# Second layer of an eight-stage transformer stack: order of the values' tiles, their copies, two weight blocks and the rotation of the shared keys

## The reference, cut to what matters

```python
def mla_layer(x, norm_g, w_in, q_a_norm, w_uq, kv_a_norm, w_ukv, q_head_norm, k_head_norm, w_out):
    proj = rms_norm(x, norm_g) @ w_in            # 1024 -> 256 + 128 + 64 + 1024
    q_lat, kv_lat, k_pe, gate = ...
    q = (rms_norm(q_lat, q_a_norm) @ w_uq).reshape(B, S, 8, 192)
    kv = (rms_norm(kv_lat, kv_a_norm) @ w_ukv).reshape(B, S, 8, 256)
    k_nope, v = kv[..., :128], kv[..., 128:]
    k = concatenate([k_nope, k_pe for every head])
    q, k = rms_norm(q, q_head_norm), rms_norm(k, k_head_norm)
    q, k = rope on the last 64 of 192 columns
    o = causal_softmax_attention(q, k, v, 1.0 / sqrt(192))
    return x + (o * silu(gate)) @ w_out
```

## Time and profile before

| | us |
|---|---|
| median of 3 runs | 1969.71 (1968.24 to 1970.51) |
| the profiled execution, its own time | 1964.89 |
| its span (first to last instruction) | 1963.1 |
| TensorE busy in it | 1867.9 (95%) |
| VectorE, ScalarE, POOL busy | 967.3, 794.3, 467.8 |
| mean granted TensorE clock | 0.979 |

### The profile page before, as it was taken

One profiled execution on the slowest core, in us unless ns is written; L12 is line 12 of the kernel. 1 busy time (PEld: TensorE's weight loads), 2 busy tenths in 40 slices (PEclk: granted clock), 3 DMA queues, 4 the chain that ended last, 5 costly groups with the idle time before them and its releaser, 6 DMA issues.

```text
span 1963.1 us, 24562 instructions
## 1 busy us (share of the span) xinstructions
PE 1867.9 (95%) x9682; PEld 1465.6 (75%) x9682; DVE 967.3 (49%) x1575; ACT 794.3 (40%) x1397; POOL 467.8 (24%) x471
## 2 busy tenths in 40 slices
PE   6999989999999989999999999999998999999997
PEld 5987777765677756667888888877877788888885
DVE  5345564575446577744533333354555353333334
ACT  4235663454435355554442323233444334232322
POOL 0035551101312124541120201005556302010200
PEclk9999999998999989999999999999999799999998
DMA  4321111221012310001223222221111023222231
GB/s 152 97 76 52 49 38 56 88 72 54 1 54 84 124 54 23 23 23 54 87 97 103 98 87 96 97 86 54 65 55 55 23 86 107 97 95 98 88 103 66
DMA packets 40289, 143.32 MB, mean 73 GB/s; under 512 B 4592, under 2 KB 4976, under 8 KB 40176
## 3 DMA queue, kind: packets, MB, share of 16 engines
q1 hardware_dynamic: 40176, 141.76, 21.9%
HBM read 139.64 MB, written 2.10 MB: 72 GB/s over the span
## 4 chain that ended last, share of the span: by engine, by line
PE 85%; DVE 5%; ACT 4%; POOL 3%; issue 2%; DMA 1%; DVEq 0%; SPq 0%; ACTq 0%; POOLq 0%
PE BANK L275 22%; PE BANK L277 21%; PE BANK L276 21%; PE BANK L856 3%; PE BANK L629 2%; PE BANK L1618 2%; PE BANK L1575 1%; PE BANK L1599 1%; ACT WH L252 1%; PE BANK L913 1%; DVE LH L719 1%; PE BANK L2357 1%; PE BANK L614 1%; PE BANK L2382 1%; PE BANK L2304 1%
## 5 line engine op out<-in xcount | busy, mean ns | idle before, releaser
L252 ACT ACTIVATE WH<-WRAW 128x1024 fp32r<-128x1024 f32 x262 | 273.5, 1045 | 487.2 <-PE BANK L277 448.3
L261 DVE TENSOR_TENSOR WL<-WRAW,WH 128x1024 fp32r<-128x1024 f32 (+1 forms) x249 | 325.2, 1306 | 269.8 <-ACT WH L252 269.7
L275 PE MATMUL BANK<-HH,WH 128*128 128x512 f32 x1048 | 426.5, 407 | 20.8 <-DVE WL L261 18.1
L277 PE MATMUL BANK<-HL,WH 128*128 128x512 f32 x1048 | 410.1, 391 | 0.0
L276 PE MATMUL BANK<-HH,WL 128*128 128x512 f32 x1048 | 409.7, 391 | 0.0
L275 PEld LDWEIGHTS BANK<-HH,WH 128*128 128x128 f32 x1048 | 197.8, 189 | 71.1 <-ACT WH L252 18.8
L276 PEld LDWEIGHTS BANK<-HH,WL 128*128 128x128 f32 x1048 | 198.1, 189 | 43.1 <-issue 5.3
L277 PEld LDWEIGHTS BANK<-HL,WH 128*128 128x128 f32 x1048 | 197.6, 189 | 42.5
L2245 POOL TENSOR_TENSOR HID<-TMP,HID 128x512 fp32r<-128x512 f32 x64 | 83.0, 1297 | 532.4 <-ACT HID L2226 532.4
L277 PE MATMUL BANK<-HID,WH 128*128 128x512 f32 x512 | 202.2, 395 | 0.0
L275 PE MATMUL BANK<-HID,WH 128*128 128x512 f32 x512 | 202.2, 395 | 0.0
(11 more groups left out here) (387 smaller groups left out, 3153.4 us busy)
## 6 DMA issues: line engine op xcount, KB each, us to landing
WRAW<-in_w SPq DMA_DIRECT2D x77, 512.0 KB, 3.4
WRAW<-in_wu SPq DMA_DIRECT2D x64, 512.0 KB, 3.2
WRAW<-in_wd SPq DMA_DIRECT2D x64, 512.0 KB, 3.2
WRAW<-in_w0o SPq DMA_DIRECT2D x8, 512.0 KB, 3.4
WRAW<-in_w1o SPq DMA_DIRECT2D x8, 512.0 KB, 3.5
WRAW<-in_wc SPq DMA_DIRECT2D x8, 512.0 KB, 3.3
WRAW<-in_w2o SPq DMA_DIRECT2D x8, 512.0 KB, 3.2
WRAW<-in_w3o SPq DMA_DIRECT2D x8, 512.0 KB, 3.3
```

Source lines behind the costliest of these rows:

```text
L252: e.activation(WH[b % NS][:, 0:n], WRAW[b % NR][:, 0:n], ACT.Copy).then_inc(*inc("s_high", ("high", b)))
L261: e.tensor_tensor(WL[b % NS][:, 0:n], WRAW[b % NR][:, 0:n], WH[b % NS][:, 0:n].bitcast(F32), ALU.subtract).then_inc(*inc("s_low_pool" if p ...
L275: e.matmul(dst, ah, bh, start=first and i == 0, stop=False)
L277: made = e.matmul(dst, ah, bl, start=False, stop=last and i == len(sets) - 1)
```

## The change

Six edits, all in the second layer.

1. `k rot` holds bank 7 in place of the ring's next, and the ring is one of seven banks from there on (before: from the first query tile on). All tiles behind it lie one bank further back than before.
2. VectorE turns the shared keys (`rope(("k",), ...)`) after the four evictions of `queries(0)` in place of before the evictions of the key tiles.
3. The values' tiles hold banks 0 to 7 in their own order; the ring's count is moved by 13 in place of 4, so that the output tiles lie where they lay.
4. VectorE copies the values' tiles 0, 2, 4 and 6, ScalarE 1, 3, 5 and 7, after the silus and the table load.
5. The splits of `m_o` 1 and `m_o` 2 move from ahead of the attention steps to the end of their steps 9 and 13, on both engines.
6. The first product with the values waits for the copies of tiles 6 and 7, as there are two copying engines now.

```diff
+        m_late = {9: "m_g", 13: "m_v"}
...
-            bank, was = banks.take("k rot", ("k sin",))
+            bank, was = banks.hold("k rot", 7, ("k sin",))
+            banks.ring = range(7)
...
-            banks.ring = range(7)
             queries(0)
...
-                    bank, was = banks.take(("m_v", 2 * i + half), ("evac", "m_v", 2 * i + half))
+                    bank, was = banks.hold(("m_v", 2 * i + half), 2 * i + half, ("evac", "m_v", 2 * i + half))
...
-            banks.i += 4
+            banks.i += 13
...
                     if step == 7:
+                        w.wait_ge(*at("evac", "m_v", 6))
                         w.wait_ge(*at("evac", "m_v", 7))
...
-            rope(("k",), "k rot", mkpe)
             for m in range(0, 8, 2):
                 w.wait_ge(*at("tile", "m_k", m))
                 e.tensor_copy(mkn[:, m, :], banks["m_k", m]).then_inc(*inc("s_evac", ("evac", "m_k", m)))
...
             queries(0)
+            rope(("k",), "k rot", mkpe)
             gate(2)
...
-            gate(7)
-            for m in range(8):
+            by_rs(e, w, "m_g", 7, mlg[:, 7, :])
+            for m in range(0, 8, 2):
                 w.wait_ge(*at("tile", "m_v", 7 if m == 6 else m))
-                e.tensor_copy(mv[:, m // 2, 512 * (m % 2):512 * (m % 2) + 512], banks["m_v", m]).then_inc(
-                    *inc("s_evac", ("evac", "m_v", m)))
-            split_low(e, w, after_block("m_v", 0), False)
+                e.tensor_copy(mv[:, m // 2, 0:512], banks["m_v", m]).then_inc(*inc("s_evac", ("evac", "m_v", m)))
...
+                if step in m_late:
+                    split_low(e, w, after_block(m_late[step], 7 if step == 9 else 0), False)
...
-            split_high(e, w, after_block("m_g", 7))
             silu(7)
             e.preload_act_table_set("natural_log_exp_and_others")
-            split_high(e, w, after_block("m_v", 0))
+            for m in range(1, 8, 2):
+                w.wait_ge(*at("tile", "m_v", m))
+                e.activation(mv[:, m // 2, 512:1024], banks["m_v", m], ACT.Copy).then_inc(
+                    *inc("s_evac_act", ("evac", "m_v", m)))
...
+                if step in m_late:
+                    split_high(e, w, after_block(m_late[step], 7 if step == 9 else 0))
```

## The result

| | before | after |
|---|---|---|
| median us | 1968.97 (4 runs, 1968.16 to 1970.51) | 1958.90 (4 runs, 1957.71 to 1960.55) |
| ratio | | 0.9949, 95% interval 0.9931 to 0.9966 |
| the profiled execution, its own time; span | 1964.89; 1963.1 | 1960.55; 1958.8 |
| mean granted clock | 0.979 | 0.979 |

The change makes the kernel 10 us faster, 0.5%; 8.8 us were forecast, with a time of 1961.0 us. In a later session it measured 1959.50 us (11 runs), ratio 0.9956, interval 0.9940 to 0.9972.

A forecast was written before the change was run, and what follows sets the result against it. TensorE, busy for 95% of the span, was taken to lose time only by standing still and by the lower clock. 0.9 + 1.2 + 6.7 = 8.8 us won gave 1961.0 us, 8-in-10 range 1956.5 to 1968.2.

The forecast's parts named there:

- What bounds it: Second layer's attention: TensorE stalls 1.52 us ahead of the scores, then runs 13.5 us at granted clock 0.50.
- Rotation and key tiles: Ahead of the first query tile: a 2.38 us stall goes, 0.6 and 0.9 us waits come; 0.9 us won.
- Values' tiles: Ahead of the first scores: the 1.52 us stall goes, the second tile loses 0.3 us; 1.2 us won.
- Clock: In the first scores: without the stall the clock stays at 1.00, halving 13.5 us of work; 6.7 us won.
- Late splits: At attention steps 9 and 13: the moved splits hide behind TensorE's other work; cost 0, bounds 0 to 0.5 each.
- Sum: Whole kernel: 0.9 + 1.2 + 6.7 = 8.8 us won, for a time of 1961.0 us.
- rule on bank cycling: Rival at the key tiles: the new waits cost the clock, giving 1962.6 or 1967.7 us; chance 0.10.
- The rival of later stalls: Stalls after this stage come 8.8 us earlier and together lose over 4 us of clock; chance 0.06.

The follow-up runs named there:

- `p2_values`: Before, with values' tiles on banks 0 to 7, copied by VectorE and ScalarE; both splits still ahead of the steps: 1958.57 us, ratio 0.9948.
- `p3_late`: Before, with only the two splits moved to the end of steps 9 and 13; banks and VectorE's eight copies unchanged: 1959.41 us, ratio 0.9960.
- `p4_fill`: Before, plus seven bf16 matmuls of 512 columns, changing no result, in the stall ahead of the scores: 1959.68 us, ratio 0.9958.
- `q3_stall2`: Changed kernel with a 1.9 us stall put back ahead of the scores, by two further copies on ScalarE: 1967.19 us, ratio 1.0006.
- `q1_nokeys`: Changed kernel with the rotation product back on the ring of eight and the shared keys turned before the key copies: 1960.47 us, ratio 0.9969.
- `p1_keys`: Before, with only the rotation product on bank 7, the ring of seven and the later turning of shared keys: 1966.64 us, ratio 0.9990.
- `q2_stall0`: Changed kernel with a 0.7 us stall ahead of the scores, waiting for the copy of values' tile 7: 1958.91 us, ratio 0.9952.
- `s1_both9`: Changed kernel with both late splits at step 9 instead of steps 9 and 13: 1958.24 us, ratio 0.9960.
- `r_after`: The changed kernel once more, unaltered, beside its variants on one chip: 1959.50 us, ratio 0.9956.
- `b2_early`: Changed kernel, ring shifted so no tile of the layer's first half lies on a late-evicted bank, splits back ahead of the steps: 1953.33 us, ratio 0.9920.

## Why the prediction was right

- **What bounds it.** The stall of 1.52 us is bank 0's wait for the sixth copy, and the low clock hangs on the stall. Both held: `p2_values` and `p3_late` take the stall away by different means, `p4_fill` leaves the wait and takes only the idleness, and `q3_stall2` puts a stall back and loses the clock again.
- **Rotation and key tiles: 0.9 forecast, 0.9 measured.** The new waits were put at 0.6 and 0.9 us; the trace has 0.51 and 0.87. The first query tile comes 1.41 - 0.51 = 0.90 us earlier.
- **Values' tiles: 1.2 forecast, 1.4 measured.** The stall of the second tile cost 0.25 us, not 0.3 (`q1_nokeys`, where it is not, is 0.25 shorter), and the whole of 1.52 us went with some 0.1 more.
- **Clock: 6.7 forecast, 6.4 measured** in the traced executions (83.23 to 76.84), 6.3 by filling alone.
- **Late splits: 0, measured 0.** The last length is 76.84 us with them and 76.83 without (`p2_values`). The forecast put the copy of unit 4 at 1.0 us ahead of its product; it ends 1.15 us ahead.
- **Sum: 8.8 forecast, 8.7 in the stage.** The medians say 10.1 in one session and 7.6 in another. The rest may lie in other layers or in how long before's low stretch lasts: 13.5 us in its trace, 20 us in `p1_keys` behind the same stall, which costs 3.2 us more. How the timed executions of before divide between these was not seen, so that the medians scatter to both sides of 8.8 tests the sum no further than to some 1.5 us. (By its own terms the forecast is 1969.71 - 8.8 = 1960.9 us, not 1961.0.)
- **The absolute times.** It put query tile 0 near 394.5, the first scores near 469.4 and the last product 8.8 us earlier; they came at 397.35, at 472.07 and 5.8 us earlier. All of this traced execution runs 2.85 us late from the first layer on. Only the lengths could be forecast.
- **A thing it left half open.** It booked the 1.2 us under edits 3, 4 and 6, but its working also takes the split away from in front of the copies, which is edit 5. The experiments show that either would have been enough, so the gain of the whole is not the sum of its parts.
- **The rivals.** The Trainium skill's rule on bank cycling (page "TensorE: Matmul & The Clock Gate", section "A second HAM failure mode: psum-queue depth-cycling") could make the two small stalls at the key tiles swing the clock. In the trace of the changed kernel they did not: 1.00 from 389.67 to 398.00 in the window shown. Five more traces have the same two stalls (`p1_keys`, `q2_stall0`, `q3_stall2`, `s1_both9`, `r_after`), and all have 1.00 behind them up to 405 us. One row that the prediction took for a bank stall is none: in the 1.50 us at 867.00 TensorE waits for a tile that POOL scales. The rival of later stalls is real in single executions (762 us in the trace of after) and too small there to change the sign.

## What to carry to other kernels

Read a stretch at half clock together with the stall ahead of it: here 1.5 us of waiting cost 8 us, and the list of waits shows only the 1.5. Where a stall stands just before work of this kind (here float32 scores, 128 to 512 wide and half of them on 64 rows), remove it by the order of banks, or fill it with matmuls whose result is overwritten. That it is the kind of work behind the stall that decides was not tested. When comparing two traces, compare lengths between two marks of the same stage, as stalls elsewhere win and lose the clock from one execution to the next.

## What was not expected of the hardware

- **The low stretch lasts with TensorE busy.** It lasted 13.5, 20 and 24 us behind stalls of 1.5, 1.5 and 1.9 us, with TensorE listed as fully busy in float32 scores, while behind the stall of the first query tile in `p3_late` the clock was back after some 3 us of triple passes.
- **A stall's length does not decide alone.** 2.38 us ahead of the first query tile kept the clock in before's trace, 2.4 us at the same place lost it in that of `p3_late`, one of the five traces that have this stall. The Trainium skill (page "TensorE: Matmul & The Clock Gate", section "What's actually happening") says that the chip's watch on activity runs free of the kernel's start. The traces fit that: in the identical first layer one stall of 2.8 us, which ends near 140 us, lost the clock in seven of the fourteen traces (after, `p2_values`, `b2_early` among them) and not in the others (before, `p3_late`). So a single trace does not tell whether a stall is harmless.
